# Expert weights of a mixture-of-experts layer in packets of 32,768 bytes, read by TensorE with a step of four

## The reference

```python
N_EXPERTS, TOP_K, D_EXPERT = 32, 2, 512     # D_MODEL = 2048
def expert_block(args):
    xe, e = args                                        # rows of one expert, and its number
    a = jax.nn.silu((xe @ w_e_gate[e]).astype(jnp.float32))   # w_e_gate[e]: 2048 x 512
    b = (xe @ w_e_up[e]).astype(jnp.float32)                  # w_e_up[e]:   2048 x 512
    return ((a * b).astype(xe.dtype) @ w_e_down[e]).astype(jnp.float32)   # w_e_down[e]: 512 x 2048
```

## Time and profile before

| | us |
|---|---|
| Profiled execution, its own time | 1556.78 |
| Its span, first to last instruction | 1555.0 |
| Median of three runs | 1555.86 |
| PE busy | 1249.6 |
| PE weight loads busy | 648.6 |
| DVE busy | 501.3 |
| ACT busy | 194.1 |

### The profile page before, as it was taken

One profiled execution on the slowest core, in us unless ns is written; L12 is line 12 of the kernel. 1 busy time (PEld: TensorE's weight loads), 2 busy tenths in 40 slices (PEclk: granted clock), 3 DMA queues, 4 the chain that ended last, 5 costly groups with the idle time before them and its releaser, 6 DMA issues.

```text
span 1555.0 us, 23502 instructions
## 1 busy us (share of the span) xinstructions
PE 1249.6 (80%) x10063; PEld 648.6 (42%) x10063; DVE 501.3 (32%) x1042; ACT 194.1 (12%) x465; POOL 59.6 (4%) x111
## 2 busy tenths in 40 slices
PE   7989999999999997786776766776776776677677
PEld 4444468766878764332222222222322222222222
DVE  2300165740103314333323323323332432332333
ACT  3200012311111323010000000000000000000000
POOL 2000022221100000000000000000000000000000
PEclk9999999998999998899998898899898998999898
DMA  9999999979998998799999999999999999999997
GB/s 355 367 367 363 307 329 391 363 256 389 380 398 327 368 403 314 323 400 426 428 426 425 427 427 424 427 427 425 427 427 425 426 429 425 425 428 428 423 428 311
DMA packets 114030, 608.85 MB, mean 392 GB/s; under 512 B 11198, under 2 KB 14421, under 8 KB 79785
## 3 DMA queue, kind: packets, MB, share of 16 engines
q1 hardware_dynamic: 72027, 479.04, 74.8%
q10 hardware_dynamic: 34550, 100.80, 17.9%
q0 software_dynamic: 7408, 28.37, 5.2%
HBM read 603.16 MB, written 106.18 MB: 456 GB/s over the span
## 4 chain that ended last, share of the span: by engine, by line
DMA 51%; PE 42%; DVE 2%; issue 1%; ACTq 1%; SPq 1%; ACT 1%; POOL 0%; DVEq 0%
DMA ring<-in_w_e_up_dram 46%; PE pb L1135 10%; PE pb L654 10%; PE pb L740 4%; PE pb L899 4%; DMA ring<-in_w_out_dram 2%; PE pb L917 2%; PE pb L682 2%; DMA ring<-in_w_cq_dram 2%; PE pb L1026 1%; PE pb L660 1%; SPq L489 1%; DMA ring<-Z 1%; PE pb L858 1%; PE pb L868 1%
## 5 line engine op out<-in xcount | busy, mean ns | idle before, releaser
L1135 PE MATMUL pb<-ring,xT 128*32 128x256 f32 x4096 | 311.5, 471 | 196.6 <-DMA ring<-in_w_e_up_dram 191.2
L1135 PEld LDWEIGHTS pb<-ring,xT 128*32 128x32 f32 x4096 | 154.1, 134 | 377.1 <-DMA ring<-in_w_e_up_dram 240.7
L2012 DVE TENSOR_TENSOR Z<-pb,Z 128x512 f32<-128x512 f32 x248 | 153.6, 681 | 339.7 <-PE pb L1090 339.7
L654 PE MATMUL pb<-ring,hreg 128*128 128x512 f32 (+1 forms) x320 | 128.5, 562 | 4.0 <-issue 4.0
L1165 PE MATMUL pb<-ring,xT 128*32 128x512 f32 x960 | 109.2, 595 | 0.0
L1090 PE MATMUL pb<-xT 32*128 32x512 f32 x744 | 102.9, 623 | 0.0
L1066 PE MATMUL pb<-Z,xT 128*32 128x512 f32 (+1 forms) x768 | 95.1, 609 | 3.0 <-DVE xT L1990 3.0
L654 PEld LDWEIGHTS pb<-ring,hreg 128*128 128x128 f32 x320 | 61.4, 193 | 68.0 <-issue 66.3
L899 PE MATMUL pb<-hreg,ring 128*128 128x264 f32 x320 | 78.7, 404 | 2.8 <-DMA ring<-in_w_out_dram 2.8
L740 PE MATMUL pb<-hreg,ring 128*128 128x264 f32 x320 | 75.3, 395 | 0.2 <-DMA ring<-in_w_in_dram 0.2
L1506 ACT ACTIVATE xT<-pb 128x128 f32<-128x128 f32 x32 | 8.9, 277 | 523.9 <-PE pb L1135 523.9
(11 more groups left out here) (331 smaller groups left out, 1121.9 us busy)
## 6 DMA issues: line engine op xcount, KB each, us to landing
ring<-in_w_e_gate_dram SPq DMA_DIRECT2D x63, 2048.0 KB, 19.0
ring<-in_w_e_up_dram SPq DMA_DIRECT2D x63, 2048.0 KB, 23.5
ring<-in_w_e_down_dram SPq DMA_DIRECT2D x30, 4096.0 KB, 22.1
out_win_k_sample_dram<-in_cache_win_k_dram ACTq DMA_DIRECT2D x24, 1536.0 KB, 14.8
out_win_v_sample_dram<-in_cache_win_v_dram ACTq DMA_DIRECT2D x24, 1536.0 KB, 14.3
ring<-in_w_in_dram SPq DMA_DIRECT2D x7, 4096.0 KB, 29.7
ring<-in_w_out_dram SPq DMA_DIRECT2D x4, 4096.0 KB, 33.2
out_win_k_sample_dram<-in_cache_win_k_dram ACTq DMA_DIRECT2D x8, 1488.0 KB, 15.5
```

The costliest lines, as they stand in the source:

```text
L654: last = mm(bk[:, 0:n], xt[:, k, tile * P:tile * P + P], w[:, k, 0:n], start=(k == 0), stop=(k == KT - 1))
L1135: last = mm(pb[1][32 * c:32 * c + 32, 0:256], XT[:, k % 4, 32 * (k // 4):32 * (k // 4) + 32], w[:, :, k8, P * c:P * c + P], start=(k == 0) ...
L2012: last = V.tensor_tensor(d, banks[c][:, :], d, ALU.add)
```

## The change

Half 0 of the ring now holds all of gate and half 1 all of up, each loaded by one DMA in which a partition's share is one run of 32,768 bytes. Down is loaded with row 4 p + k on partition p, again one run of 32,768 bytes per partition. So that the hidden rows come in the order that down now has, block c of the products takes the columns 4 n + c: the moving operand is 128 elements at a step of four (16 bytes), of gate in the first half and of up in the second. One product of 256 columns becomes two of 128. The semaphores count one DMA per half instead of two. Expert 31's half 1 is still cut in two pieces, now k = 0 to 7 and k = 8 to 15 of up, and its down in four.

```diff
             def gate_up(i, e, half):
-                for m in range(2):
-                    w = a[("w_e_gate", "w_e_up")[m]][0]
-                    src = w[e] if isinstance(i, int) else w[bass.ds(e, 1)].rearrange("o k n -> (o k) n")
-                    sp.dma_start(ring[:, half, 4096 * m:4096 * m + 4096].rearrange("p (k n) -> p k n", k=8),
-                                 src.rearrange("(p k) n -> p k n", k=KT)[:, 8 * half:8 * half + 8, :])\
-                        .then_inc(gu_landed[half], 16)
+                w = a[("w_e_gate", "w_e_up")[half]][0]
+                src = w[e] if isinstance(i, int) else w[bass.ds(e, 1)].rearrange("o k n -> (o k) n")
+                sp.dma_start(ring[:, half, :].rearrange("p (k n) -> p k n", k=KT), src.rearrange("(p k) n -> p k n", k=KT))\
+                    .then_inc(gu_landed[half], 16)
             def down(i, e):
...
-                sp.dma_start(slot2.rearrange("p (k n) -> p k n", k=4), src.rearrange("(k p) n -> p k n", p=P))\
+                sp.dma_start(slot2.rearrange("p (k n) -> p k n", k=4), src.rearrange("(p k) n -> p k n", k=4))\
                     .then_inc(dn_landed, 16)
...
+            src = a["w_e_up"][0][NE - 1].rearrange("(p k) n -> p k n", k=KT)
             for q in range(2):
-                for m in range(2):
-                    src = a[("w_e_gate", "w_e_up")[m]][0][NE - 1].rearrange("(p k) n -> p k n", k=KT)
-                    at = 4096 * m + 2048 * q
-                    sp.dma_start(ring[:, 1, at:at + 2048].rearrange("p (k n) -> p k n", k=4), src[:, 8 + 4 * q:12 + 4 * q, :])\
-                        .then_inc(gu_landed[1] if q else quarter_landed, 16)
+                sp.dma_start(ring[:, 1, 4096 * q:4096 * q + 4096].rearrange("p (k n) -> p k n", k=8), src[:, 8 * q:8 * q + 8])\
+                    .then_inc(gu_landed[1] if q else quarter_landed, 16)
...
-                    w = ring[:, half, :].rearrange("p (m k n) -> p m k n", m=2, k=8)
-                    for k8 in range(8):
-                        if in_two and k8 == 4:
-                            pe.wait_ge(gu_landed[1], 32 * (i + 1))
-                        k = 8 * half + k8
+                    w = ring[:, half, :].rearrange("p (k n c) -> p k c n", k=KT, c=4)
+                    for k in range(KT):
+                        if in_two and k == 8:
+                            pe.wait_ge(gu_landed[1], 16 * (i + 1))
                         for c in range(4):
-                            last = mm(pb[1][32 * c:32 * c + 32, 0:256], XT[:, k % 4, 32 * (k // 4):32 * (k // 4) + 32],
-                                      w[:, :, k8, P * c:P * c + P], start=(k == 0), stop=(k == KT - 1))
+                            last = mm(pb[1][32 * c:32 * c + 32, P * half:P * half + P], XT[:, k % 4, 32 * (k // 4):32 * (k // 4) + 32],
+                                      w[:, k, c, :], start=(k == 0), stop=(k == KT - 1))
```

More of the change, by code:

```diff
@@ L504, in expert_weights @@
                 down(i, e)
-            w1 = a["w_e_down"][0][1].rearrange("(k p) n -> p k n", p=P)
+            w1 = a["w_e_down"][0][1].rearrange("(p k) n -> p k n", k=4)
             piece_used(sp, CQ)
@@ L525, in _ @@
             sp.wait_ge(gu_used[1], NE - 1)
+            src = a["w_e_up"][0][NE - 1].rearrange("(p k) n -> p k n", k=KT)
             for q in range(2):
-                for m in range(2):
-                    src = a[("w_e_gate", "w_e_up")[m]][0][NE - 1].rearrange("(p k) n -> p k n", k=KT)
-                    at = 4096 * m + 2048 * q
-                    sp.dma_start(ring[:, 1, at:at + 2048].rearrange("p (k n) -> p k n", k=4), src[:, 8 + 4 * q:12 + 4 * q, :])\
-                        .then_inc(gu_landed[1] if q else quarter_landed, 16)
+                sp.dma_start(ring[:, 1, 4096 * q:4096 * q + 4096].rearrange("p (k n) -> p k n", k=8), src[:, 8 * q:8 * q + 8])\
+                    .then_inc(gu_landed[1] if q else quarter_landed, 16)
             sp.wait_ge(dn_used, NE - 1)
-            w = a["w_e_down"][0][NE - 1].rearrange("(k p) n -> p k n", p=P)
+            w = a["w_e_down"][0][NE - 1].rearrange("(p k) n -> p k n", k=4)
             for q in range(4):
@@ L1127, in expert @@
                     in_two = last_of_all and half == 1
-                    pe.wait_ge(*((quarter_landed, 32) if in_two else (gu_landed[half], 32 * (i + 1))))
-                    w = ring[:, half, :].rearrange("p (m k n) -> p m k n", m=2, k=8)
-                    for k8 in range(8):
-                        if in_two and k8 == 4:
-                            pe.wait_ge(gu_landed[1], 32 * (i + 1))
-                        k = 8 * half + k8
+                    pe.wait_ge(*((quarter_landed, 16) if in_two else (gu_landed[half], 16 * (i + 1))))
+                    w = ring[:, half, :].rearrange("p (k n c) -> p k c n", k=KT, c=4)
+                    for k in range(KT):
+                        if in_two and k == 8:
+                            pe.wait_ge(gu_landed[1], 16 * (i + 1))
                         for c in range(4):
-                            last = mm(pb[1][32 * c:32 * c + 32, 0:256], XT[:, k % 4, 32 * (k // 4):32 * (k // 4) + 32],
-                                      w[:, :, k8, P * c:P * c + P], start=(k == 0), stop=(k == KT - 1))
+                            last = mm(pb[1][32 * c:32 * c + 32, P * half:P * half + P], XT[:, k % 4, 32 * (k // 4):32 * (k // 4) + 32],
+                                      w[:, k, c, :], start=(k == 0), stop=(k == KT - 1))
                     last.then_inc(gu_used[half], 1)
@@ L1179, in _ @@
             with pe.If(n_over > 0):
-                pe.wait_ge(quarter_landed, 32)
+                pe.wait_ge(quarter_landed, 16)
                 for landed in last_landed[0:3]:
```

## The result

In 18 runs each the changed kernel took a median of 1575.71 us and the kernel before 1562.3: a ratio of 1.0089 (95% interval 1.0062 to 1.0115; the two medians alone give 1.0086). Every ratio in this document compares the runs that lie within 1.5% of their kernel's fastest, which leaves out none but three of e7's twelve. The forecast was 1555 us in a range of 1540 to 1567. Of the miss of 20.7 us, 6.4 lie in the kernel before itself, whose median in these runs stands that much above the three shown. The other 14.3 are the change's, and they have the wrong sign: it costs 13.4 us where 0.9 were to be won.

The account below looks back on a forecast made before the run. The prediction took the DMA weight stream to bound 827 us: 8.4 us won by packets, less 2.2 at the start and 4.1 at the end, leaves 2.1 off 1556.78, so 1555 us, in a range of 1540 to 1567.

Parts of the forecast that it names:

- The packets: Steady weight stream: 40 fewer packets per engine at 7.5 ns save 0.30 us per expert, 8.4 us over 28 periods.
- Rival 3: Weight stream: larger packets bring nothing, period stays 29.52 us while products still cost 6.4; 1564 us; chance 12%.
- The products: Expert products: the step of four makes each half take T = 6.4 us, from line 671's 88 ns per 128 strided elements.
- rival 2: Expert products: the four strided streams collide and queue, T = 14.9 us, PE sets the period, about 1969 us; chance 20%.
- Rival 1: Expert products: the step is free, T unchanged, 1548 us, or 1539 with 14.8 ns per packet; chance 28%.
- its bound T = 8.1: Steady stream: half time from which PE's chain would bind; start loses 8.7, end 9.2 against 8.4 gained, 1566 us.
- The start: First experts: slower halves delay the load requests, so the stream runs 2.2 us later, the packets' 0.5 us included.
- the sign that the forecast named: Start of the expert part: expert 3's half 0 should land near 697 us.
- the forecast's step for the queue: Start: PE frees expert 1's half 0 late, so the DMA queue stands dry 4.0 us, from 652.2 to 656.2.
- the 2.4 us that were to go: Start: the queue's old dry spells at expert 2's half 1 and down, 0.4 and 2.0 us, should vanish.
- the forecast's chain of 13.0 + 2T: PE's work per expert: 13.0 us besides two halves of T, 25.8 us at T = 6.4, hidden under 29.22.
- The end: Last three halves, after the stream: PE's slower products give back 4.1 of the 6.2 us won, leaving 2.1.

Follow-up runs that it names:

- e7: e2 with the last expert's gate and up loaded and multiplied by halves of k, 256 columns, as in the kernel before; ratio 0.9962 from nine runs.
- e1: Changed kernel with contiguous product columns and down back in its old rows and 8 KB runs; 1559.35 us, ratio 1.001 to the kernel before.
- e2: Changed kernel with a step of two instead of four, down in two runs of 16 KB; 1556.88 us, ratio 0.9974 to the kernel before.
- e5: Changed kernel with contiguous product columns, all loads still in 32 KB runs (computes other values); 1556.64 us, ratio 0.9996 to the kernel before.
- e6: Kernel before, with only column group 0 of the expert products read at a step of four; 1573.39 us in one execution.
- e3: Kernel before, transfers untouched, its 256-column products read at a step of four (computes other values); 1580.05 us, ratio 1.0121.
- e11: Changed kernel unaltered, profiled again for the stretch ahead of the first expert load; span 1559.3 us, expert part 936.60.
- e4: Changed kernel with early loads cut: expert 0's gate and up to 16 KB runs, experts 0 and 1's down to 8 KB; 1564.29 us, ratio 1.0046.
- e9: e7 with expert 0's gate and up loaded in runs of 16 KB; 1552.79 us, ratio 0.9962 to the kernel before, over all twelve runs.

## Why the forecast was wrong, step by step

**The packets: right, and somewhat small.** Forecast 0.30 us per expert and a period of 29.22; measured 0.386 and 29.14. The price per packet is a straight line: 16 packets fewer on each engine bring 0.156 us (e1), 32 bring 0.304 (e2), 40 bring 0.386 (the changed kernel, e5). That is 9.5 to 9.8 ns each, not 7.5, and 10.8 us over 28 periods, not 8.4. Rival 3, no gain, is out.

**The products: the step that failed.** The forecast took the half's time T = 6.4 us from line 671's weight loads, 88 ns more per 128 strided elements; measured is 7.55, or (7.55 - 3.66) / 32 = 122 ns more per round. The mechanism was the one put down, a cost that each of the four streams pays side by side: e6 shows it, and rules out rival 2, in which they queue. The term was mis-sized because a stationary operand's load at a step of 16 was taken for a moving operand at a step of four. Rival 1, a free step, nearly holds for a step of two (3.90 for 3.66 to 3.70) and not for four. The Trainium skill (SBUF — State Buffer, Specifications (TRN2)) has lines of 16 bytes and asks for two hits on each for full speed. The trace agrees: with a step of two an fp32 stream hits each such line twice, with four once, and that is where the time doubles. A step of three and steps beyond four were not run, so another rule with its limit between two and four would fit as well. Four fp32 elements, which the prediction names as the limit, are no free step here.

The miss of 1.15 us in T looks small, but the steps that the forecast wrote down lean on it with 6 us per us, three at the start and three at the end: 6.9 us. (At its bound T = 8.1 they give 7.3 us for the start and 1565 in all, not the 8.7 and 1566 put down.)

**The start: forecast 2.2 us later, measured 8.2** at expert 7, with the packets' gain up to there already in it; with the old packets 10.5 (e3). At expert 3, the sign that the forecast named, it is 14 us (84.6 us after the first product for 70.4). In the forecast's own terms, the stream starts 2.2 us later (forecast 1.1), and the queue then stands dry for about 9 us (forecast 4.0; DMA share of 665 to 680 us). With T = 7.55 the forecast's step for the queue gives 6.3, and in e11, which had no dip of the clock here, it stood dry for 5 to 6. Of the 2.4 us that were to go behind it about 1 stays. The forecast had expert 1's half 0 start 23.4 us after the first product; it was 28.86. Of these 5.5 us, 2.1 are the two halves of expert 0 (14.95 for 12.8). The other 3.3 are PE's work between them at a lower clock: line 1062 took 4.39 us and line 1161 5.27, in an execution without that dip (e11) 2.89 and 3.57. No term of the forecast held this. In e4 and e11 the same half started 25.6 and 25.5 us after the first product, and their expert parts are 937.05 and 936.60. The later PE is, the later it frees the slots, and the loads behind are asked for into an empty queue. Up to expert 6 PE then paces the kernel, at 27.83 us per expert; the forecast's chain of 13.0 + 2T gives 28.1.

**The end: forecast 4.1 given back, measured 8.8.** Three halves, as forecast: 7.58, 8.87 and 7.60 us where 5.20, 6.28 and 3.66 had been, 8.9 together. With T = 7.55 the forecast's step gives 3.4 more, 7.5; most of the rest is the pause of 0.91 us that the doubled records bring (2.54 in e2, gone in e7). This pause was in no term. The trace points to the loading of instructions: in each of the eight profiles with this pause it ends 1.2 to 1.5 us after the end of a 16 KB packet on the queue whose kind is instruction, though it does not say for which engine the packet is. That queue has 38 packets in the changed kernel; before it had

```profile
q8 instruction: 34, 0.56, 0.1%
```

**The steady stream: right.** By the forecast it hides T up to about 8.1; it did at 7.55, with 1.0 us left. Larger T was not run.

**The sum.** In the expert part 8.2 - 8.9 + 8.8 = 8.1 us, where the forecast had 2.1 won; four executions confirm it (936.6 to 938.95 against 930.3 and 930.6). Of these 10.2 us T alone makes 6.9 by the forecast's steps, the dip of the clock about 2 (938.35 to 938.95 with it, 936.6 without) and the pause 0.9; the 2.4 that were to go leave 1, the packets' larger gain takes 2.4 off, and about 2 are not placed.

The medians differ by 13.4 and 13.7 us in the two sets of runs, 5 us more. That part stays open. It is not a fixed cost of the large early runs of gate and up: e5 has them and no delay, e9 has them cut and a delay of 7 us (87.9 us from first score product to first expert product, 80.9 in e5). The early loads of down are a rival that no run tests alone, and the profiles point to it. In the six whose early down comes in runs of 8 KB (the two of the kernel before, e1, e3, e4, e6) this stage took 79.7 to 80.9 us five times and 84.3 once; in the eight with 16 or 32 KB (the changed kernel's four, e2, e5, e7, e9) it took 80.8 and 80.9 in two and 82.9 to 89.9 in six, 3.8 us more in the mean. The timed runs lean the same way: outside the expert part the medians stand 5 us above the kernel before's in the changed kernel and 1.9 to 8.5 in the others with long runs of down (e2, e5, e9, and e7 over all its runs), against -1.7 to 3.3 in e1, e3 and e4, each uncertain by 2 to 3 us. The stretch ahead of that stage varies by more than 5 us from execution to execution, and the timed runs leave no trace.

That the time lies within 1%, to which the forecast gave 70%, is luck: the gain and the loss in the expert part came out as 8.9 and 17.0 us, where 8.4 and 6.3 were written down. And with 18 runs of each kernel a difference of 0.9% is told from none, which the prediction doubted.

**A version that beats both.** e7 and e9 keep what the larger runs bring with a step that costs little. Their expert parts are 920.55 and 920.09 us, 10 less than before. Of the whole time e9 shows 0.9962 of the kernel before, with an interval just under 1; e7 shows it only without its three longest runs.

## What to carry to other kernels

Before a layout makes TensorE read fp32 at a step, measure that step as a moving operand: every second element nearly kept the speed here (3.90 us for 3.66), every fourth halved it (7.55), and one slow column group of four was enough. Work that the stream hides in the steady part is paid in full where nothing hides it, at the ramp and the tail, so put an uncertain duration through those two places first and see how many times it counts. Here each packet saved brought the same 9.5 to 9.8 ns up to runs of 32 KB, and the mixed form at a step of two (down in runs of 16 KB) kept 0.304 of 0.386 us per expert.

## What was not expected of the hardware

- A read at a step of four hardly feels the clock: the last expert's first 73 records took 62 ns each (4.54 us, at a granted clock of 0.62 over just these) where full clock gives 59, while a contiguous half goes from 3.66 to 6.28 us at 0.58. In the kernels with the step of four PE is also busy for more of the span (1424.7 us here for 1249.6 before), and the mean granted clock of their profiles is 0.979 to 0.987, where it is 0.929 to 0.934 in every other.
- Straight-line code on either side of the loop can stall PE. The last expert's half of 128 records was held up after the 73rd in every kernel that has them (0.83 to 2.57 us), and in none that has 64. Expert 1's half 0, ahead of the loop, was held up before its last record in all five kernels with 128 faster records (e1, e2, e5, e7, e9: 1.21 to 2.69 us). Each of these pauses ends 1.2 to 1.5 us after a 16 KB packet of the instruction queue; that queue has 38 packets, 36 in e7 and e9, and 34 in the kernels with 64 records.
- Under the same program, the 530 to 550 us ahead of the first expert load differ by up to 18 us between executions of one kernel.
